# A hybrid mLSTM, S5 and expert layer: opening reordered, GLU spread over the first head's projections, a wait for stores moved

## The reference

```python
xs = x_sample + pos2d(...)                        # positions on the latent tokens only
mod = silu(c) @ w_ada + b_ada                     # 6 x 1024 values: shift, scale, gate, twice; one set per stream
h = rmsnorm(x, norm_mix) * (1 + scale1) + shift1
q, k, v, o, gates, u, ga, gb = split(h @ w_in)
hm = (mlstm_fwd(q, k, v, gates) + flip(mlstm_bwd(...))) * sigmoid(o)
h_a = rmsnorm_per_head(hm) * head_norm            # 4 heads x 256
z = s5_fwd(u) + flip(s5_bwd(flip(u))) + s5_d * u  # 32 groups x 16 channels, 64 complex states
h_b = gelu(z) * sigmoid(z @ w_glu + b_glu)        # GLU, width 512
x = x + gate1 * ((sigmoid(ga) * (h_a @ w_pA) + sigmoid(gb) * (h_b @ w_pB)) @ w_out)
h = rmsnorm(x, norm_ffn) * (1 + scale2) + shift2
aff = softmax(h @ w_router + b_router)            # 16 experts, each takes its best 64 latent and 16 context tokens
y = scatter_add(silu(xe @ w1) * (xe @ w3) @ w2 * topv)   # hidden width 1536
x = rmsnorm(x + gate2 * y, norm_final)
```

## Time and profile before

| | |
|---|---|
| median of 3 runs | 1861.05 us (1856.96 to 1862.49) |
| profiled execution | 1856.57 us, span 1854.7 us |
| PE busy | 1689.7 us (91% of the span) |
| DVE busy | 570.0 us (31%) |
| ACT busy | 374.7 us (20%) |
| POOL busy | 100.4 us (5%) |
| opening block | 0 to 63.9 us, PE busy 31.1 us of it |
| gates and u | 63.9 to 111.8 us, PE busy 46.8 us, POOL busy 33.5 us |
| S5 block | 111.8 to 309.3 us |
| experts, first gather to last matmul | 1033.5 to 1823 us |

### The profile page before, as it was taken

One profiled execution on the slowest core, in us unless ns is written; L12 is line 12 of the kernel. 1 busy time (PEld: TensorE's weight loads), 2 busy tenths in 40 slices (PEclk: granted clock), 3 DMA queues, 4 the chain that ended last, 5 costly groups with the idle time before them and its releaser, 6 DMA issues. The chain is left out here.

```text
span 1854.7 us, 33663 instructions
## 1 busy us (share of the span) xinstructions
PE 1689.7 (91%) x15258; PEld 960.7 (52%) x15258; DVE 570.0 (31%) x1313; ACT 374.7 (20%) x777; POOL 100.4 (5%) x95
## 2 busy tenths in 40 slices
PE   5799998999999898968995699999999999999993
PEld 2366665546446464668883234444444444444441
DVE  5369991011213131347646001111111111111113
ACT  3343332121121313145434100000000000000001
POOL 1610000000000000000000000000000000000000
PEclk9799998999999999989998799999999999999997
DMA  9244455010202012043314799999999999999963
GB/s 396 77 110 169 154 182 230 12 46 1 102 12 103 11 47 79 15 157 123 139 69 193 277 355 384 403 401 402 400 403 405 408 404 404 406 400 405 407 255 128
DMA packets 56916, 420.61 MB, mean 227 GB/s; under 512 B 10932, under 2 KB 17588, under 8 KB 26948
## 3 DMA queue, kind: packets, MB, share of 16 engines
q1 hardware_dynamic: 49188, 386.97, 52.7%
q0 software_dynamic: 6864, 28.85, 5.2%
q10 hardware_dynamic: 720, 2.62, 0.3%
HBM read 391.86 MB, written 24.42 MB: 224 GB/s over the span
## 5 line engine op out<-in xcount | busy, mean ns | idle before, releaser
L1737 PE MATMUL bank<-place,x 128*32 128x384 f32 x3120 | 258.1, 489 | 0.9 <-ACT x L1800 0.9
L1737 PE MATMUL bank<-ring_tail,x 128*32 128x384 f32 x3024 | 249.8, 488 | 1.4 <-issue 1.4
L1737 PEld LDWEIGHTS bank<-place,x 128*32 128x32 f32 x3120 | 100.4, 110 | 147.3 <-issue 143.8
L1737 PEld LDWEIGHTS bank<-ring_tail,x 128*32 128x32 f32 x3024 | 98.2, 110 | 145.1 <-issue 143.8
L1831 DVE SCALAR_TENSOR_TENSOR hT<-bank,gvr,xT 32x256 f32<-32x256 f32 (+1 forms) x192 | 92.1, 480 | 241.3 <-PE bank L1767 238.7
L1845 DVE TENSOR_TENSOR hid<-sq,bank 128x384 f32<-128x384 f32 x48 | 23.7, 550 | 446.8 <-issue 362.3
L1089 PE MATMUL bank<-place,hT 128*128 128x512 f32 x320 | 138.0, 592 | 0.0
L239 PE MATMUL bank<-hT,xT 128*128 128x512 f32 x256 | 132.7, 600 | 1.1 <-ACT qk L249 0.9
L1767 PE MATMUL bank<-place,hidT 128*32 128x256 f32 x2304 | 128.0, 379 | 0.0
L1767 PE MATMUL bank<-ring_tail,hidT 128*32 128x256 f32 x2304 | 127.8, 379 | 0.0
L1438 PE MATMUL bank<-a_h,w_h 128*128 128x320 f32 x320 | 101.2, 316 | 19.4 <-DVE w_l L1510 16.9
(11 more groups left out here) (364 smaller groups left out, 1905.4 us busy)
## 6 DMA issues: line engine op xcount, KB each, us to landing
place<-w_e_dram SPq DMA_DIRECT2D x97, 1536.0 KB, 11.6
ring_tail<-w_e_dram SPq DMA_DIRECT2D x95, 1536.0 KB, 11.7
place<-w_ada_dram SPq DMA_DIRECT2D x12, 2048.0 KB, 9.1
xT<-w_gate_dram POOLq DMA_DIRECT2D x8, 1024.0 KB, 6.5
place<-w_qk_dram SPq DMA_DIRECT2D x4, 2048.0 KB, 8.9
place<-w_vo_dram SPq DMA_DIRECT2D x4, 2048.0 KB, 10.7
place<-w_pAB_dram SPq DMA_DIRECT2D x4, 1536.0 KB, 7.9
hT<-gates_dram SPq DMA_DIRECT2D x4, 1280.0 KB, 6.1
```

What stands on the lines that cost most here:

```text
L1737: mm = pe.matmul(PS[bank + j][TJ * g:TJ * g + TJ, 0:FC], x[:, e % 2, 2 * c + k, TJ * j:TJ * j + TJ], w[:, k, FC * g:FC * g + FC], start=(c ...
```

## The change

Three edits, and two that follow from them.

1. *Opening.* On the sync queue the constants, the input and the positions come ahead of all adaLN pieces. The pieces are taken in the order shift low half, scale low half, shift high half, scale high half (`ADA = [0, 2, 1, 3]`), so that the first four feature blocks can be modulated before the last two pieces; the gain is computed in two halves. PE does the mean square first, then four adaLN pieces in four banks. On DVE the position adds stand in the middle of the S5 coefficients, and the wait for the constants behind their first part. The six GpSimd products for `bb` move to the next block, behind its loads and ahead of its coefficient tables.
2. *GLU.* Its block is gone. `zT`, `w_glu` and the sigmoids live in buffers of the mLSTM block that are not yet in use. PE turns z in banks 4 to 7, begins head 0, and does two GLU columns after q tile 0 and two after q tile 1. GELU writes straight into `hbT`.
3. *Router.* ACT no longer waits at the block's end for the residual rows' stores; the first `scatter` does.
4. The heads' pieces start in slot 0 instead of slot 1; the first is loaded in the S5 block once the last additions are done, ahead of the store of the final states. The ring's places in `place` are reordered to match.
5. `xrow` stays allocated through the experts; `hid` and `hidT` move into `xT`, and the gathered activations are padded to 96 columns instead of 128.

```diff
-            plan.append((src, freed_by, value, (1 + len(plan) - CH_H) % NSLOT))
+            plan.append((src, freed_by, value, (len(plan) - CH_H) % NSLOT))
...
+        ADA = [0, 2, 1, 3] + list(range(4, 12))
...
-                load_weights(sp, 1)
                 sp.dma_start(consts[:], ar["consts"]).then_inc(sem("consts_in"), 16)
-                load_weights(sp, 2)
                 sp.dma_start(xT[:], ar["xT"]).then_inc(sem("x_in"), 16)
                 sp.dma_start(posT[:], ar["posT"]).then_inc(sem("x_in"), 16)
-                load_weights(sp, 3)
-                sp.dma_start(s5bc[:], ar["s5bc"]).then_inc(sem("s5bc_in"), 16)
-                load_weights(sp, 4)
+                load_weights(sp, 2)
...
+                load_weights(sp, 3)
+                sp.dma_start(s5bc[:], ar["s5bc"]).then_inc(sem("s5bc_in"), 16)
+                load_weights(sp, 4)
                 load_weights(sp, CH_U + 1)
...
-                act_ada(act, 0, 0)
-                act_ada(act, 1, 1)
                 for k in range(KD):
                     act.wait_ge(sem("x_pos"), k + 1)
                     act_square(act, 0, k)
+                act_ada(act, 0, 0)
                 act_rms(act, 0, tmp)
-                act_ada(act, 2, 0)
-                act_ada(act, 3, 1)
-                act_modulate(act, 0, hT)
+                act_ada(act, 1, 1)
+                act_ada(act, 2, 2)
+                act_modulate(act, 0, hT, (0, 1))
+                act_ada(act, 3, 3)
+                act_modulate(act, 0, hT, (2, 3, 4, 5, 6, 7))
...
+                pe.wait_ge(sem("meanw_set"), 1)
+                pe_mean_square(pe, 0)
                 pe.wait_ge(sem("c_silu"), 1)
                 pe.wait_ge(sem("sel4_set"), 1)
-                pe_ada(pe, 0, 0)
-                pe_ada(pe, 1, 1)
-                pe.wait_ge(sem("meanw_set"), 1)
-                pe_mean_square(pe, 0)
-                for c in (2, 3):
-                    pe.wait_ge(sem("mod_in"), c - 1)
-                    pe_ada(pe, c, c % 2)
+                for c in range(4):
+                    pe_ada(pe, c, c)
...
+                dve_inverse_mean(dve, v, 0, tmp)
                 dve_ada(dve, 0, 0)
                 dve_ada(dve, 1, 1)
...
+                dve_gain(dve, 0, PC_NMIX, 0, 4).then_inc(sem("gain_ready"), 1)
+                dve_normalise(dve, 0, (0, 1, 2, 3))
+                dve_ada(dve, 2, 2)
+                dve_ada(dve, 3, 3)
                 dve.wait_ge(sem("mod_in"), 4)
-                dve_gain(dve, 0, PC_NMIX).then_inc(sem("gain_ready"), 1)
-                dve_normalise(dve, 0)
+                dve_gain(dve, 0, PC_NMIX, 4, KD).then_inc(sem("gain_ready"), 1)
+                dve_normalise(dve, 0, (4, 5, 6, 7))
...
                 for half in range(2):
                     load_gate(pool, half)
                 p = chain(pool, "pool")
+                pool.wait_ge(sem("s5bc_in"), 16)
+                pool.wait_ge(sem("s5_step"), 3)
+                wr = bc(bfac[:, 0, :].unsqueeze(2), [P, GN, GC])
+                wi = bc(bfac[:, 1, :].unsqueeze(2), [P, GN, GC])
+                pool.tensor_tensor(tb[:, 0], s5bc[:, 0], wr, ALU.mult)
+                p(pool.tensor_tensor(tb[:, 1], s5bc[:, 1], wi, ALU.mult))
+                p(pool.tensor_tensor(bb[:, 0], tb[:, 0], tb[:, 1], ALU.subtract))
+                pool.tensor_tensor(tb[:, 0], s5bc[:, 0], wi, ALU.mult)
+                p(pool.tensor_tensor(tb[:, 1], s5bc[:, 1], wr, ALU.mult))
+                p(pool.tensor_tensor(bb[:, 1], tb[:, 0], tb[:, 1], ALU.add))
                 coefficients_in(pool, p, 0)
...
-                    load_weights(sp, CH_A + 2 * q + 3)
+                    load_weights(sp, CH_A + 2 * q + 3 if q + 1 < NQ else CH_H)
+                sp.wait_ge(sem("s5_v_done"), 4 * NQ)
+                load_weights(sp, CH_H + 1)
                 sp.wait_ge(sem("xfin_ready"), NQ)
...
                     for m in range(4):
+                        if h == 0 and m:
+                            for x in (() if m == 3 else (2 * m - 2, 2 * m - 1)):
+                                glu(x)
                         u = 9 * h + m
                         proj_wait(u)
...
+                for b in range(8):
+                    turn_z(b)
                 proj_qk(0)
                 proj_vo(0)
...
-        SLOTS = (12288, 15360, 0, 4096, 8192)
+        SLOTS = (12288, 15360, 8192, 0, 4096)
...
-                for x in range(2):
-                    act.wait_ge(sem(f"xrow_out{x}"), 16 * ((NT + 1 - x) // 2))
...
                 def scatter(e):
                     pool.wait_ge(sem("y_ready"), e + 1)
+                    if e == 0:
+                        for r in range(2):
+                            pool.wait_ge(sem(f"xrow_out{r}"), 16 * ((NT + 1 - r) // 2))
```

More of the change, by code:

```diff
@@ L280, in act_rms, with dve_normalise @@
             act.activation(rsb[:], tmp[:], ACT.Sqrt).then_inc(sem("rms"), 1)
-        def dve_normalise(dve, n):
+        def dve_normalise(dve, n, ks=range(KD)):
             dve.wait_ge(sem("rms"), n + 1)
-            for k in range(KD):
+            for k in ks:
                 if k >= 2:
@@ L353, in _ @@
                 pool.memset(meanw[:], 1.0 / D).then_inc(sem("meanw_set"), 1)
[L354 to L364, removed]
             @block.scalar
@@ L455, in _ @@
                          bc(pw[:, 0, m:m + 1, :], [P, m, GN]), bc(pw[:, 1, m:m + 1, :], [P, m, GN]), t4(m))
+                dve.wait_ge(sem("consts_in"), 16)
+                dve.tensor_reduce(sel4[:], ident.rearrange("p (g x) -> p x g", g=4)[:, 0:2, :], AX.X,
+                                  ALU.add).then_inc(sem("sel4_set"), 1)
+                dve.wait_ge(sem("x_in"), 32)
+                for k in range(KD):
+                    dve.tensor_tensor(xT[:, k, 0:LAT], xT[:, k, 0:LAT], posT[:, k], ALU.add).then_inc(sem("x_pos"), 1)
                 F, B = slice(0, SP_), slice(SP_, P)
@@ L1064, in proj_wait, with turn_z, glu @@
                         pe.wait_ge(sem("proj_copied"), u - 1 + (u - 2 + 5) // 9)
+                def turn_z(b):
+                    if b >= 4:
+                        pe.wait_ge(sem("z_in"), b - 3)
+                    for i in range(4):
+                        mm = pe.transpose(PS[4 + b % 4][:, i * J:(i + 1) * J],
+                                          zC[:, 4 * (b % 2) + i, (b // 2) * P:(b // 2 + 1) * P], ident[0:J, 0:J])
+                    mm.then_inc(sem("z_turned"), 1)
+                def glu(m):
+                    if m == 0:
+                        pe.wait_ge(sem("wglu_in"), 16)
+                        pe.wait_ge(sem("z_in"), 8)
+                    if m >= 2:
+                        pe.wait_ge(sem("glu_sig"), m - 1)
+                    for k in range(4):
+                        w = wgl[:, k, m * P:(m + 1) * P]
+                        pe.matmul(PS[4 + m % 2][:, :], w, zT[:, k, 0:LAT], start=(k == 0), stop=(k == 3))
+                        mm = pe.matmul(PS[6 + m % 2][:, 0:CTX], w, zT[:, k, LAT:TOK], start=(k == 0), stop=(k == 3))
+                    mm.then_inc(sem("glu_done"), 1)
                 def proj_qk(h):
@@ L1187, in _, with glu_sigmoid @@
                 a = chain(act, "act")
+                def glu_sigmoid(m):
+                    act.wait_ge(sem("glu_done"), m + 1)
+                    if m >= 2:
+                        act.wait_ge(sem("hb_ready"), m - 1)
+                    b = par[:, PC_BGLU + m:PC_BGLU + m + 1]
+                    act.activation(sg[:, m % 2, 0:LAT], PS[4 + m % 2][:, :], ACT.Sigmoid, bias=b)
+                    act.activation(sg[:, m % 2, LAT:TOK], PS[6 + m % 2][:, 0:CTX], ACT.Sigmoid,
+                                   bias=b).then_inc(sem("glu_sig"), 1)
                 def out_qk(h):
                     for m in range(4):
+                        if h == 0 and m in (1, 2):
+                            for x in (2 * m - 2, 2 * m - 1):
+                                glu_sigmoid(x)
                         u = 9 * h + m
@@ L1254, in finish @@
                         act.activation(Co[:, n, :], PS[6 + n % 2][:, 0:DH + 1], ACT.Copy).then_inc(sem("co_ready"), 1)
+                act.wait_ge(sem("z_in"), 8)
+                for m in range(4):
+                    act.activation(hbT[:, m, :], zT[:, m, :], ACT.Gelu_apprx_tanh).then_inc(sem("gelu"), 1)
                 out_qk(0)
```

121 lines of the change are left out of this document (40 added, 81 removed).

## The result

The changed kernel takes 1842.16 us (median of 4 runs, 1837.43 to 1844.41) against 1861.22 (4 runs, 1856.96 to 1862.49): 19.1 us less, ratio 0.9894, 95% interval 0.9864 to 0.9923. In a later comparison it took 1841.43 (6 runs) against 1860.52 (11 runs), ratio 0.9899 (0.9881 to 0.9917). It is faster by 1.1%. The forecast was 1845 with 1833 to 1855, and the direction and range held.

A forecast was written before the change was run, and what follows sets the result against it. Experts' weight streaming beside TensorE bounds the kernel; only gaps ahead shrink: 7.6 - 7.3 - 1.5 + 6.1 + 5.4 + 4.3 = 14.6 us off 1856.6 gives 1842, put at 1845, nearer the median; range 1833 to 1855.

The forecast's parts named there:

- The gates block: Gates and u stage: the moved bb products delay GpSimd, DVE's critical chain alternates with it, barrier 7.3 us later.
- a lock: Gates stage: shared port pair held exclusively for a whole instruction, so DVE waits out GpSimd's; loss 7.3 us.
- a split: Gates stage: shared port bandwidth, DVE doing 2.8 us of work in GpSimd's 7.0; loss 4.3 us instead.
- S5's slow start: Start of the S5 stage: TensorE stands 7 us and meets it at the low clock; loss 1.5 us.
- End of S5: Barrier after S5: the final states' store goes out earlier, so the sync queue's 6.7 us wait goes; gain 6.1 us.
- GLU: Block start to head 0: copies, GELU, sigmoids and barrier hidden beside q tiles; gain 5.4 us, between 3.8 and 6.9.
- Router: Router to experts: first gather issued 7.6 us earlier but landing late in full DMA engines; gain 4.3 us.
- Opening: Up to the first barrier: inputs land 9.9 us earlier, adaLN pieces 2 and 3 at low clock; gain 7.6 us.
- (b): Rival: DVE and GpSimd hardly meet or u hides it, opening keeps its clock; near 1835 us, chance 0.2.
- (c): Rival: low clock in opening and GLU, gather late, 9 us lost in gates stage; 1855 us, chance 0.2.
- (d): Rival: the experts' weight stream takes over, each piece slowed 0.27 us by the new layout; 1867 us, chance 0.03.
- (e): Rival: the change does not do what it says, the states' store being late anyway; 1851 us, chance 0.02.

The follow-up runs named there:

- f1: Changed kernel with the six GpSimd products for bb back in the opening block: 1834.36 us (4 runs), ratio to before 0.984.
- f2: Changed kernel with the six products for bb done twice in the gates block: 1847.18 us (4 runs), ratio to before 0.992.
- g1: Changed kernel with bb back in the opening, last first-weight pieces and norm weights behind the first gather, xpos store before w_u: 1828.35 us, ratio to before 0.9834.
- g3: The changed kernel unedited, profiled a third time: 1840.23 us.
- e2: Kernel before with only the heads' weights starting in slot 0, the first loaded ahead of the final states' store: 1852.36 us, ratio 0.9956.
- e3: Kernel before with only the GLU spread over head 0, without the new slots: 1857.25 us (10 runs), ratio 0.9978.
- f3: Changed kernel with expert pieces 8 and 9 and the norm weights issued behind the first gather: 1837.32 us, ratio to before 0.9856.
- g2: The changed kernel unedited, profiled a second time: 1841.43 us (6 runs).

## Why the prediction was right, and where its steps were off

**The gates block (predicted -7.3, found -7.1).** The mechanism is right, shown by f1, f2 and g1: GpSimd holds up DVE's chain, and TensorE waits for it. The size is right by two parts that were not in the sum as such. The chain came 5.9 us later, not 7.3, and TensorE waited 4.8 us, not "some 7", since its own products at the block's start ran at the low level for longer; the other 1.3 us are the transposes at the low level. The scan of 3.52 us against 1.27 shows DVE waiting for the rest of a GpSimd instruction and then running at its own speed. The 5.9 us lie between the 7.3 of a lock and the 4.3 of a split; it is these single instructions that decide. The Trainium skill (SBUF — State Buffer, "SBUF: two separate sides") calls the shared port pair a lock held for a whole instruction; by that rule, the trace agrees.

**S5's slow start (-1.5, found -1.3): right in the number, not shown as a mechanism.** I took it that TensorE's wait would make S5 begin at the low level. It began there before as well (1.94 us for the first eight products in both kernels). Nor does the stage follow the wait: 12.4 us of waiting in f2 gave 191.0 us, 2.5 in f1 190.9, 6.0 in g3 191.0, 4.8 in the first profile 192.1, and before had 190.8. The changed kernel alone spreads over 191.0 to 192.1. Only g1 is clearly shorter (189.7 us); its first eight products took 1.07. But in e2 they took 1.23, with no wait for the rows, and the stage 191.2.

**End of S5 (+6.1, +6.2) and GLU (+5.4, +5.1).** Right. e2 and e3 show them apart from each other, by their traces 5.8 and 5.0. The new cost of GLU, taken half way between 21.0 and 24.1, was 22.9: 4.0 us of turns, 17.3 of GLU's products and 1.6 for the first q tile's start at the low level.

**Router (+4.3, +3.5).** Right within 0.8. Between "lands with the end of the backlog" (gain 3.3) and "gets its share" (5.3) the first was nearer, and f3 shows the reason: 3.7 us of the 7.8 are other transfers. The Trainium skill (DMA: Bandwidth & Descriptors, "Queues, rings and completion order") has each DMA engine take turns between its queues; a gain nearer 7, which I had worked out from it, did not come, so whatever turns the gather had, most of the backlog went ahead of it.

**Opening (+7.6, found +11.7, and +13.8 to +14.5 in nine further executions): the mis-sized term.** "Pieces 2 and 3 get 3.64 each" was wrong for one of them: only the third ran low (3.61), the fourth was back at 1.92, which is 1.7 us; the turns took 1.05 us each, not 1.5 to 1.9, some 1.5 us over the last three. The last 0.9 is a quicker way from the last piece to the last modulate, which ended at 51.9 for the 56.0 predicted. I had taken "clock was lost at that distance" from one place of one profile. In the other nine executions with this opening it was lost at no piece. In g2 and g3, the changed kernel again, the opening ended at 49.6 and 50.1: even my upper bound (gain 12.1) was passed, by up to 2.2 us, and the gates block was 1.2 and 0.3 us longer in exchange, where GpSimd's wait for the store ended after the barrier.

**The heads (0, found -5.9): not in the sum at all.** I had no term for stages that the change does not touch. In the pair of profiles it took back a third of the other terms' 18.1 us, and between the medians it did not show: they differ by 19.1. That the two profiles differ by 12.1, near the 14.6 forecast, is luck: the opening's +4.1 and the heads' -5.9 met. Before's profile, 1856.57 us at a mean granted clock of 0.962, is near the fastest of all its runs in these comparisons (1856.32 at 0.962 to 1869.08 at 0.949). So I read the 4.5 us between profile and median as that profile's short low-clock stretches; its other runs have no trace that would show it. With the opening sized right the sum would have been 18.7, and that off the median of 1861.05 gives 1842.

**The rivals.** (b), 1835 by DVE and GpSimd not meeting, is refuted for the lock but right on the opening's clock. (c), (d) and (e) did not come: GLU and gather gave 8.6 together, no piece of the weight stream was late (791.8 in both), and the store was not late.

## What to carry to other kernels

When an edit moves work from an engine's idle time into another stage, price it by what that stage's other engines share with it, and ask what the faster stage will now arrive ahead of: here f1 and g1 show that first GpSimd's products and then a 2.5 MB store stood there, worth 4 to 5 and 3 us by the traces (block and S5 together). Count DMA issues that only pass time ahead of a transfer on the critical path; two pieces and a norm vector issued behind the gather instead of ahead of it cost nothing and gave 3.7 by the trace. And read a difference of two single profiles stage by stage against their busy times: a stage with the same instructions, the same DVE and ACT and a longer TensorE time is longer by the clock. Whether the edit has a hand in that takes several profiles of both kernels.

## What was unexpected of the hardware

- A one-input DVE instruction over 4x1280 values waited for GpSimd as the two-input ones do (2.69 us for 0.81, f2).
- The same kernel's heads took 618.6 and 624.1 us in two executions with the same instructions. Over runs, time and mean granted clock go together: the changed kernel 1837.42 at 0.965 to 1844.56 at 0.959, before 1856.32 at 0.962 to 1869.08 at 0.949.
- A gather on its own queue took 4.1 us with the DMA share at 0.40 (f3), 7.8 beside the last pieces ahead of the experts, and 12.6 in the full stream.
